# The feed-forward half of a hybrid encoder layer: the up-projection as seven block products, the down-projection as a stage of its own

## The reference, cut to what matters

```python
def conv_ffn(h, w_up, conv_w, conv_b, w_down, conv_state):
    L = h.shape[1]
    a, b = jnp.split(h @ w_up, 2, axis=-1)
    ext = jnp.concatenate([conv_state.astype(a.dtype), a], axis=1)
    conv = conv_b[None, None, :] + sum(ext[:, j:j + L] * conv_w[j] for j in range(CONV_W))
    y = (jax.nn.silu(conv) * b) @ w_down
    return y, ext[:, L:]
...
    x = x + g1[:, None, :] * mix
    h2 = modulate(rmsnorm(x, ln2), sh2, sc2)
    ffn, conv_new = conv_ffn(h2, w_up, conv_w, conv_b, w_down, conv_state)
    x = x + g2[:, None, :] * ffn
```

## Time and profile before

| | |
|---|---|
| time, median of 3 runs | 1400.57 us (1399.63 to 1401.8) |
| span of the profiled execution | 1399.1 us |
| TensorE busy | 1311.4 us, 94% of the span |
| VectorE, ScalarE, GpSimd busy | 769.9, 449.0, 470.5 us |
| feed-forward part on TensorE | from 562.4 to 1376.5 us |
| up products in the loop (L1502) | 3024 matmuls, 504.1 us |
| down products (L1545) | 1560 matmuls, 258.2 us |
| moved by DMA | 102.39 MB |

### The profile page before, as it was taken

The page is one execution under the profiler, slowest core; times in us unless marked ns, Lnnn a source line. Parts: engine busy times, 40 slices in busy tenths (PEclk is TensorE's granted clock), DMA queues, the critical chain, the costliest instruction groups (busy, mean ns, idle before and its releaser), DMA issues.

```text
span 1399.1 us, 21647 instructions
## 1 busy us (share of the span) xinstructions
PE 1311.4 (94%) x7911; PEld 1246.1 (89%) x7911; DVE 769.9 (55%) x1450; ACT 449.0 (32%) x980; POOL 470.5 (34%) x321
## 2 busy tenths in 40 slices
PE   5579999999999999899999999999999999999993
PEld 2468888988989898699999999999999999999992
DVE  6967558376486798542526252525343444434358
ACT  5464434344346314632121212121212212121225
POOL 4752122131233465633222222222222223141434
PEclk9799999999999999899999999999999999999997
DMA  9412223032133452111111111111111111120103
GB/s 367 143 40 87 69 70 120 28 111 95 70 108 110 156 171 85 31 46 46 46 46 47 46 45 46 46 46 46 46 45 43 50 31 60 32 61 30 32 1 128
DMA packets 37615, 102.39 MB, mean 73 GB/s; under 512 B 4704, under 2 KB 16288, under 8 KB 37408
## 3 DMA queue, kind: packets, MB, share of 16 engines
q1 hardware_dynamic: 35872, 100.52, 21.9%
q10 hardware_dynamic: 1664, 0.72, 0.2%
...
## 4 chain that ended last, share of the span: by engine, by line
issue 46%; PE 26%; POOL 12%; DVE 12%; ACT 3%; DMA 1%; POOLq 0%; DVEq 0%; SPq 0%; ACTq 0%; PEldq 0%
PE bank L1224 14%; POOL w_hl L718 7%; POOL u_hl L829 3%; DVE ada_out L883 3%; DVE ada_w L883 2%; PE bank L1502 2%; PE bank L1336 1%; DVE std L1070 1%; POOL act_hl L735 1%; PE bank L1306 1%; PE bank L1321 1%; DVE std L902 1%; DMA xm<-in_x_t 1%; PE bank L1370 1%; PE bank L1373 1%
## 5 line engine op out<-in xcount | busy, mean ns | idle before, releaser
L1502 PE MATMUL bank<-act_hl,w_hl 128*128 128x362 f32 (+1 forms) x3024 | 504.1, 328 | 3.4 <-issue 3.4
L718 POOL TENSOR_TENSOR w_hl<-w_raw,w_hl 128x1024 fp32r<-128x1024 f32 x96 | 237.5, 2475 | 801.7 <-ACT w_hl L398 801.7
L1502 PEld LDWEIGHTS bank<-act_hl,w_hl 128*128 128x128 f32 x3024 | 502.1, 188 | 4.6 <-issue 4.6
L1224 PE MATMUL bank<-act_hl,w_hl 128*128 128x362 f32 (+1 forms) x1656 | 306.1, 336 | 0.1
L1224 PEld LDWEIGHTS bank<-act_hl,w_hl 128*128 128x128 f32 x1656 | 272.8, 189 | 9.3 <-issue 7.1
L1545 PE MATMUL bank<-u_hl,w_hl 128*128 128x362 f32 (+1 forms) x1560 | 258.2, 326 | 1.0 <-DVE xm L1142 1.0
L1545 PEld LDWEIGHTS bank<-u_hl,w_hl 128*128 128x128 f32 x1560 | 254.1, 188 | 4.6 <-issue 2.9
L1142 DVE SCALAR_TENSOR_TENSOR xm<-bank,mod,xm 128x298 f32<-128x298 f32 (+2 forms) x352 | 167.5, 498 | 94.3 <-PE bank L1545 90.5
L398 ACT ACTIVATE w_hl<-w_raw 128x1024 fp32r<-128x1024 f32 x96 | 100.9, 1052 | 227.6 <-PE bank L1502 205.0
L1120 DVE TENSOR_SCALAR conv<-gate_ext,conv_wb_sb 128x1090 f32<-128x1090 f32 x22 | 18.7, 849 | 266.9 <-ACT conv_out L660 266.9
L653 ACT ACTIVATE gate_ext<-bank 128x364 f32<-128x364 f32 (+1 forms) x88 | 32.5, 397 | 203.2 <-PE bank L1502 201.6
...
## 6 DMA issues: line engine op xcount, KB each, us to landing
w_raw<-in_w_units SPq DMA_DIRECT2D x96, 512.0 KB, 3.5
ada_w<-in_w_ada_t SPq DMA_DIRECT2D x52, 512.0 KB, 3.6
...
xm<-in_x_t SPq DMA_DIRECT2D x1, 1456.0 KB, 10.2
...
```

The source lines that it names most:

```text
L718: pool.tensor_tensor(w_hl[:, slot, 1], w_raw[:, slot], w_hl[:, slot, 0].bitcast(F32), ALU.subtract).then_inc(wl_ready, 1)
L1224: ins = pe.matmul(bank[c][:, 0:m], w_hl[:, slot, w, k, :], act_hl[:, x, k, a:a + m], start=(pas == 0 and i == 0), stop=(pas == 2 and i == ...
L1502: ins = pe.matmul(bank[c][:, 0:m], w_hl[:, slot, w, k, :], act_hl[:, x, k, a:a + m], start=(pas == 0 and k == 0), stop=(pas == 2 and k == ...
```

## The change: what it does

**Up-projection.** Per inner tile f the weights form a 2 by 2 matrix of blocks: gate and up unit by the two halves of the 1024 inputs (a block is 512 by 128). The activations form a 2 by 2 matrix too: input half by token quarter pair. The 1088 tokens are taken as two halves of 544, each as two columns of 272 (`HC`). Instead of eight block products per half, seven are made, of the Strassen kind in Winograd's form: of sums of blocks (S1 to S4 of the weights, T1 to T4 of the activations), each with 4 blocks of 128 by 3 passes, so 12 matmuls of 272 columns. VectorE forms S1 to S4 per f (`block_sums`) and T1 to T4 once per half (`x_sums`, `x_last_sum`); ScalarE and GpSimd split the seven weight blocks per f (`block_hi`, `block_lo`), in a ring of 13; the seven activation blocks of each half are split once (`x_hi`, `x_lo`) and stay in SBUF. Three of the seven accumulate onto a bank that holds an earlier product; the results are put together by VectorE out of PSUM (`up_evac`).

**u and x in DRAM.** x before the feed-forward is stored to DRAM and loaded back for the residual; u is stored per f (`store_u`).

**Down-projection.** After all of u, six passes: three token chunks by two halves of the 1024 outputs. A pass has 22 steps, one per f: it loads half a weight unit (128x512) and one chunk of u, splits both, and does 4 output tiles by 3 matmuls into four banks which accumulate over the pass. The final norm of the first two chunks runs under later passes. Loops are unrolled.

```diff
+HC = 272
+RING = 13
+PRODUCTS = 7
+A_SRC = ("A11", "S2", "S3", "S1", "A12", "A22", "S4")
+X_SRC = ("B11", "T2", "T3", "T1", "B21", "T4", "B22")
+PSUM_OF = (0, 1, 2, 3, 0, 2, 3)
+X_LO_POOL = (0, 2, 4)
+X_LO_DVE = (1, 3, 5, 6)
+U_RING = 4
+G_DOWN = 6
...
+            for f in range(FT):
+                for j in (2 * f + 3, 2 * f + 4):
+                    if j < 2 * FT:
+                        load_raw(j)
+                if f > 0:
+                    store_u(f - 1)
+
+            def load_down(q):
+                g, f = divmod(q, FT)
+                a, n = CHUNKS[g // 2]
+                if q < 6:
+                    sp.wait_ge(bl_ready, PRODUCTS * FT)
+                else:
+                    sp.wait_ge(dl_ready, q - 6 + 1)
...
+                if q < U_RING:
+                    sp.wait_ge(product, 2 * PRODUCTS * FT - PRODUCTS)
+                else:
+                    sp.wait_ge(ul_ready, q - U_RING + 1)
...
+            for q in range(G_DOWN * FT):
+                g, f = divmod(q, FT)
+                load_down(q)
+                if q == 3:
+                    store_u(FT - 1)
+                    sp.wait_ge(ext_ready, FT)
+                    sp.dma_start(p_conv, conv_out[:, :, :]).then_inc(stored, 16)
+                if q in (8, 10, 12):
+                    load_residual((q - 8) // 2)
...
+            def down_hi(q):
+
+                g, f = divmod(q, FT)
+                n = CHUNKS[g // 2][1]
+                act.wait_ge(dw_loaded[q % 6], 16 * (q // 6 + 1))
...
+                    act.wait_ge(down_step, q - 6 + 1)
+                act.activation(w_blocks[:, q % 6, 0], raw_halves[:, q % 6], ACT.Copy).then_inc(dh_ready, 1)
+                act.wait_ge(du_loaded[q % U_RING], 16 * (q // U_RING + 1))
+                if q >= U_RING:
+                    act.wait_ge(down_step, q - U_RING + 1)
+                act.activation(u_hl[:, q % U_RING, 0, 0:n], u_raw[:, q % U_RING, 0:n], ACT.Copy).then_inc(uh_ready, 1)
...
+            for q in range(G_DOWN * FT):
+                g, f = divmod(q, FT)
+                if q == 2:
+                    silu(FT - 1)
+                down_hi(q)
+                if g > 0 and f in (1, 2, 3, 4):
+                    k = 4 * ((g - 1) % 2) + f - 1
+                    final_square((g - 1) // 2, k)
+                if g in (2, 4):
+                    c = g // 2 - 1
+                    if f == 7:
+                        final_root(c)
...
+            def block_lo(f, i):
+
+                q = PRODUCTS * f + i
+                pool.wait_ge(bh_ready, q + 1)
+                pool.tensor_tensor(w_block(q)[:, 1], a_source(f, i), w_block(q)[:, 0].bitcast(F32),
+                                   ALU.subtract).then_inc(bl_ready, 1)
...
+            dve.wait_ge(state_stored, 32 * HEADS + 32)
+            x_sums(0)
+            for i in (1, 3):
+                x_lo(0, i)
+            x_last_sum(0)
+            for i in (5, 6):
+                x_lo(0, i)
+            up_evac(0, 0, 0)
+            up_evac(0, 0, 1)
+            invert(17, 2)
+            x_times_inverse(2, CHUNKS[2][0], T, 2)
...
+            for f in range(FT):
+                if f > 0:
+                    convolve(f - 1)
+                    for which in range(3):
+                        up_evac(f, 0, which)
+                    gated(f - 1)
+                    up_evac(f, 0, 3)
+                    up_evac(f, 0, 4)
+                if f + 1 < FT:
+                    block_sums(f + 1)
+                for which in range(5):
+                    up_evac(f, 1, which)
...
+            for q in range(G_DOWN * FT):
+                g, f = divmod(q, FT)
+                if q == 1:
+                    convolve(FT - 1)
+                if q == 3:
+                    gated(FT - 1)
+                down_lo(q)
+                if g > 0 and f == 0:
+                    for o in range(4):
+                        down_out(g - 1, o)
...
+            def up_product(f, h, i):
+
+                q, n = PRODUCTS * f + i, bank[4 * h + PSUM_OF[i]]
+                first = i < 4
                 if h == 0:
-                    pe.wait_ge(dve_evac, 3 * N_OUT - 2 + c)
...
+                    pe.wait_ge(bl_ready, q + 1)
+                if i == 0 and f > 0:
+                    pe.wait_ge(snap, 4 * f - 4 + 2 * h + 2)
+                elif 0 < i < 4 and f > 0:
+                    pe.wait_ge(evac_up, 10 * f - 10 + 5 * h + (1, 4, 5)[i - 1])
+                elif i == 4:
+                    pe.wait_ge(snap, 4 * f + 2 * h + 1)
+                elif i > 4:
+                    pe.wait_ge(evac_up, 10 * f + 5 * h + i - 3)
...
+                    for k in range(4):
+                        ins = pe.matmul(n[:, 0:HC], w_block(q)[:, w, P * k:P * (k + 1)], x_half(h)[:, i, x, k, :],
+                                        start=(first and pas == k == 0),
...
+                for f in range(FT):
+                    q = FT * g + f
+                    pe.wait_ge(dl_ready, q + 1)
+                    pe.wait_ge(ul_ready, q + 1)
+                    for o in range(4):
+                        for pas, (w, x) in enumerate(((0, 0), (0, 1), (1, 0))):
+                            ins = pe.matmul(bank[4 * (g % 2) + o][:, 0:m], w_blocks[:, q % 6, w, P * o:P * (o + 1)],
+                                            u_hl[:, q % U_RING, x, 0:m], start=(f == pas == 0),
+                                            stop=(f == FT - 1 and pas == 2))
...
+                    if g in (2, 4) and f == 6:
+                        final_sum(g // 2 - 1)
```

845 lines of the change are left out of this document (538 added, 307 removed).

## The result

The changed kernel takes 1418.03 us (median of 4 runs, 1417.01 to 1419.23) beside 1401.18 for the kernel before in the same job: a ratio of 1.0118 with a 95% interval of 1.0106 to 1.013. It is slower, and the prediction, 1374 us and faster, was wrong. The profiled span is 1417.4 us against 1399.1.

What follows compares the result with a forecast made beforehand. TensorE, busy 94% of the span, was taken as the bound. 562.4 before the feed-forward + hand-over 61 + up 450 + down 281.5 + tail 17.5 = 1372.4 us of span, so 1374 us measured; whole range 1336 to 1415.

Steps and rivals of the forecast that it cites:

- Steady up: Up-projection, 21 tiles after the first: 127 ns per 272-column matmul, 450 us in all.
- Rival 1: Up-projection matmuls: columns alone decide, 116 ns per 272 columns, giving 1335 us; chance 0.12.
- rival 2: Up-projection matmuls: 272 columns no faster than today's spacing, at 160 ns giving 1490 us; chance 0.09.
- the cover of 1.4 us: Up-projection: VectorE's second evacuation ends at 6.2 us, before TensorE's sixth product needs it at 7.6, so no cost.
- Hand-over: From output projection to f = 1 at full pace: activation sums and splits not covered by matmuls, 61 us.
- Down: Down-projection: 1584 matmuls at 163.6 ns, 259 us, plus uncovered supply waits, 281.5 us in all.
- norm in mid-pass: Down-projection: ScalarE waits twice for the norm's sum, with a table load at least once, 7 us.
- start with residual: Down-projection: fifth step starting at 18 instead of 8, 10 us, plus residual loads between steps, 3 us.
- pass ends: Down-projection: four residual tiles on VectorE ahead of the next u split, 0.5 us by 5, 2.5 us.
- Rival 3: Down stage bound by its supply, the ring of u above all: 2.3 us per step, 1419 us; chance 0.09.
- The start: First down steps: splits and loads queue behind the last tile's work, fifth step at 18 instead of 8, 10 us.
- Tail: After the last down matmul: final norm of only one chunk and the last store, 17.5 us against 22.6.

Runs made afterwards that it cites:

- The two experiments: Changed kernel with hand-over lists reordered (1409.62 us), then also the second half's sums T1 to T3 earlier and one TensorE wait moved (1410.01 us).
- e1_norm_lag: Changed kernel with ScalarE's final-norm modulate one step later in passes 2 and 4 of the down stage: 1396.16 us, ratio 0.9969.
- e3_sp_late: Changed kernel with SyncE's last store of u after step 6's loads and residual loads at steps 16, 36 and 80: 1407.27 us, ratio 1.0043.

## Why the prediction was wrong, step by step

- **Steady up: right.** Predicted 127 ns and 450 us, measured 125.7 ns and 443.4. A matmul of 272 columns costs 12.4 ns beyond its columns, where 13.7 was carried over from the earlier trace rows. Rival 1 (116 ns) and rival 2 (160 ns) are both out; the cover of 1.4 us ahead of the sixth product held, no wait shows. The rule of columns plus 2.5 ns, which the prediction quotes from the Trainium skill ("TensorE: Matmul & The Clock Gate", section Back-to-back issue gap), is given there for the gap of a matmul by itself, and not for a stream of weight loads and matmuls as it is here.
- **Hand-over: too small in one term, 61 against 73.2.** By the trace its terms are: to the first product 10.4 (predicted 10), first half's sums and splits 21.9 (21.5), norm and modulation of the second half 11.6 (11), its sums and splits 18.4 (17), and from there to f = 1 11.0, where I had put 1.5 for the first weight block alone. I counted TensorE's last three products of the half as hidden; they can't start before a copy that ScalarE's list holds back, and they ran at the low clock. The two experiments took 9.5 us of it back by the profiles and 8 by the times.
- **Down: the step that failed, 281.5 against 320.6.** "All are below 1.96" was true and not enough. I compared each engine's sum per step with the step; I didn't follow what one step's list waits for in the other lists of the same step. Terms: regular steps 132 by 2.00, 264 (259); norm in mid-pass 29 (7); start with residual 24 (13); pass ends 3.5 (2.5). For the norm I priced only the wait for the root, not the scale and modulate that stand in 8 steps of each pass; e1_norm_lag shows that their order, not their work, cost 21 of the 29 us; the rest, 9 us, is near the 7 that I priced.
- **Rival 3 named the place** (lists through four engines, the exclusion, the norm on top), but it had 2.3 us in each step, where it was 3.44 in 16 steps and 20 us in pass 0: that its 1419 us is close to the 1418 measured is luck. What I held against it, 5 us of advance in the buffers, was no cover: buffers that lose 1.4 us per step are empty after four.
- **The start: too small.** The chain was seen (convolution, silu, gated product, SyncE at the store), 18 us for five steps against 20.7 measured to the start of step 4; priced too low were the residual loads, 3 us by my sum (with them and the store of u later, pass 0 fell by 13.5 us in e3_sp_late), and not priced at all was the clock, 6.8 us.
- **Tail: right**, 17.8 against 17.5.

The errors, 12 + 39 less 7, make the 45 us between 1372.4 and the span of 1417.4.
